# The y of a state-space layer: from four token phases on partitions to channels on partitions

## The chip, the cores and the metric

One Trainium2 chip, one of its cores. The metric is the device time of one execution in microseconds (us). Five engines of the core work beside one another and meet at semaphores: TensorE (PE, matmuls and weight loads), VectorE (DVE), ScalarE (ACT), GpSimd (POOL) and SyncE (SP, which issues the weight loads from memory).

## The reference

A streaming encoder step with two layers, for 512 prompt frames and 64 frames of a running stream (T = 576 tokens, model width 1024). Layer 0 is FFN, S5 mixer, FFN; layer 1 is FFN, differential attention, FFN; a LayerNorm stands behind each. The change touches the S5 mixer alone:

```python
def block_step(carry, u_blk):
    h_re, h_im = carry
    bu_re = jnp.einsum('gpc,btgc->btgp', bb_re, u_blk)
    ...
    _, _, hs_re, hs_im = lax.associative_scan(complex_affine_combine, (a_r, a_i, bu_re, bu_im), axis=1)
    y_blk = jnp.einsum('gcp,btgp->btgc', c_re, hs_re) - jnp.einsum('gcp,btgp->btgc', c_im, hs_im)
...
y = y.transpose(1, 0, 2, 3, 4).reshape(B, L, D_MODEL) + d_skip.astype(f32) * u
z = jax.nn.gelu(y).astype(x.dtype)
out, gate = jnp.split(z @ w_glu, 2, axis=-1)
return out * jax.nn.sigmoid(gate), h_re, h_im
```

## The kernel before, in words

**Tiles.** Activations lie with channels on partitions: `r` is 128 x 8 x 576. The tokens are worked in two halves, h = 0 with 256 tokens and h = 1 with 320. All large weight matrices pass through one numbered sequence of tiles, 128 output channels each, with K = 8 (or 7) blocks of 128 inputs. For a tile SP loads `raw` (four buffers), ACT casts it to `wh` (`act_hi`, L498, three buffers), DVE makes the rest `wl` = raw - wh (`dve_lo`, L504, three buffers), and PE does three matmuls per block (`pe_tile`, L520 to L522), 24 or 21 in all, of 256 or 320 columns. The cast and the subtraction for tile n+3 stand in ACT's and DVE's program at tile n, since a buffer is free only when PE has left it.

**Steps.** Everything else is a Python generator that is advanced by one step (`step(beside)`) behind each tile, on each engine separately; a step number is thus the same tile on all four engines, and the order on each engine is fixed by the program. `paced(work, n)` spreads a generator over n steps, `packed(work, room)` lets it run until the sizes that it yields (elements per partition plus 60 for each instruction) reach `room`, then ends the step. `idle(n)` does nothing for n steps.

**The S5 mixer** runs beside the FFN of the other token half: S5 of h = 0 beside FFN 0 of h = 1 (tiles of 320 columns), S5 of h = 1 beside FFN 1 of h = 0 (tiles of 256 columns), each behind the 12 steps of a LayerNorm. In its own steps:
- steps 0 to 3: the input is copied to `u4` with four token phases (jj) on the four partition groups of 32 (`dve_u4`, `act_u4`); the token block has BLK = 4 tokens, so there are n = 64 or 80 blocks
- steps 4 to 18: `pe_s5` multiplies block inputs (L1639), ACT copies them to `hs` (L1561)
- from step 11: `dve_scan`, the scan over the blocks on DVE (L1461 to L1472), for channel group grp = 0 and then grp = 1, each over `SCAN[h]` steps (11 for h = 0, 15 for h = 1) with `SCAN_ROOM[h]` of work in a step
- step `outputs_at(h, grp)` and the three behind it: PE makes y of one block of 128 channels, d, in each (L1656 and L1659) into bank d of the PSUM tensor `misc`. It waits for the scan (`s_sh`)
- four steps later: `dve_y` and `act_y` copy y out of PSUM to `ysb` (L1424), in 16 copies of 32 partitions, four on DVE (one in a step) and twelve on ACT (three in a step). Then ACT waits for DVE's copies (`s_yd`), does gelu on `ysb` in one instruction (L1581) and casts to `xh` (L1585); `pool_s5` makes `xl` (L1617)
- the step after the last: the gated linear unit of the mixer (`glu` tiles), which needs `xh` and `xl`.

**The y matmuls before.** For one d there are four q (32 channels each), and for each q one matmul with `tt2` on `u4` and two with `cp2` (real and imaginary) on `hs`, each with 128 stationary columns: 4 phases x 32 channels. So phase jj comes out on partitions 32jj, channel group q in columns q*n to (q+1)*n. Float32 matmuls are two instruction pairs in the trace each, so one d is 24 pairs. The moving operand of the `cp2` matmuls, `hs[:, grp, :, 0:GB, ri, 4d+q]`, takes one element out of every 32 (128 bytes apart); that of the `tt2` matmuls is contiguous.

## Time and profile before

| | |
|---|---|
| Median of 3 runs | 2335.3 us (2335.25 to 2335.64) |
| The profiled execution's own time | 2336.36 us |
| Its span in the trace | 2334.4 us |
| PE busy / weight loads (PEld) | 2247.0 / 2204.7 us |
| DVE, ACT, POOL busy | 1522.1, 1144.1, 579.9 us |
| PE clock granted, mean of the span | 0.984 of full |

The busy time of PE is the length of its matmul records, which overlap, so a busy PE need not be at its peak; but where PE is not busy nothing runs on it. Spans and shares are over the whole kernel, and the two S5 stretches (about 290 to 450 us and 590 to 815 us) have to be looked at for themselves. Durations of rows are from the start to the end of an instruction; for matmuls the distance between starts is what a stream of them costs.

### The profile page before, as it was taken

What the parts mean: (1) busy time and instruction counts of PE and PEld (TensorE: products, weight loads), DVE (VectorE), ACT (ScalarE), POOL (GpSimd) and SP (SyncE); (2) the same over time, 40 slices, a digit from 0 to 9 for tenths busy, and PEclk for the clock granted to TensorE, in tenths of its full rate; (3) what the DMA queues carried; (4) which work ended last, traced back from release to release, by engine and by line L of the source; (5) the groups of instructions that cost most, each with busy time, mean ns of one, the idle gap of its engine ahead of it and who ended that gap; (6) DMA issues with size and microseconds to landing.
All of it is one profiled execution on the core that took longest, in us unless ns stands there. A gap on an engine that the chain in (4) does not pass through costs nothing. (4 is left out here: it accounts for less than half of the span.)

```text
span 2334.4 us, 42465 instructions
## 1 busy us (share of the span) xinstructions
PE 2247.0 (96%) x17067; PEld 2204.7 (94%) x17067; DVE 1522.1 (65%) x2284; ACT 1144.1 (49%) x1923; POOL 579.9 (25%) x499
## 2 busy tenths in 40 slices
PE   8989999999998998999999999999999999899997
PEld 8989999999998998999999999999999998889997
DVE  6898768656788578444475575655687665465444
ACT  4434543555645547333365465555466554354332
POOL 2267401123211333211251123011352011141110
PEclk9999999999999999999999999999999999999999
DMA  9568675454665455555568655544555456355552
GB/s 250 166 187 239 195 218 174 128 170 132 213 215 175 139 162 145 182 152 149 149 200 277 189 159 172 154 122 137 153 155 176 136 153 184 106 152 162 145 155 79
DMA packets 705365, 391.12 MB, mean 168 GB/s; under 512 B 25001, under 2 KB 693138, under 8 KB 705170
## 3 DMA queue, kind: packets, MB, share of 16 engines
q1 hardware_dynamic: 662720, 332.44, 49.6%
q10 hardware_dynamic: 42450, 55.96, 7.2%
q8 instruction: 136, 2.23, 0.4%
q14 instruction: 59, 0.48, 0.1%
HBM read 366.53 MB, written 21.82 MB: 166 GB/s over the span
## 5 line engine op out<-in xcount | busy, mean ns | idle before, releaser
L504 DVE TENSOR_TENSOR wl<-raw,wh 128x1024 fp32r<-128x1024 f32 (+1 forms) x640 | 797.6, 1246 | 459.1 <-ACT wh L498 456.9
L520 PE MATMUL tile_ps<-xh,wh 128*128 128x256 f32 (+1 forms) x3520 | 1057.6, 300 | 26.8 <-DVE wl L504 13.7
L521 PE MATMUL tile_ps<-xl,wh 128*128 128x256 f32 (+1 forms) x3520 | 1039.2, 295 | 0.0
L522 PE MATMUL tile_ps<-xh,wl 128*128 128x256 f32 (+1 forms) x3520 | 1039.0, 295 | 0.0
L498 ACT CAST wh<-raw 128x1024 fp32r<-128x1024 f32 (+1 forms) x640 | 655.5, 1025 | 755.0 <-PE tile_ps L522 746.5
L520 PEld LDWEIGHTS tile_ps<-xh,wh 128*128 128x128 f32 x3520 | 669.9, 190 | 36.8 <-DVE wl L504 18.3
L521 PEld LDWEIGHTS tile_ps<-xl,wh 128*128 128x128 f32 x3520 | 671.1, 191 | 1.0 <-issue 0.2
L522 PEld LDWEIGHTS tile_ps<-xh,wl 128*128 128x128 f32 x3520 | 670.3, 190 | 0.0
L663 POOL TENSOR_TENSOR hl<-hf,hh 128x256 fp32r<-128x256 f32 (+1 forms) x176 | 245.1, 1392 | 1271.8 <-ACT hh L571 1271.2
L520 PE MATMUL tile_ps<-hh,wh 128*128 128x320 f32 (+1 forms) x1472 | 443.5, 301 | 7.5 <-POOL hl L663 4.3
L521 PE MATMUL tile_ps<-hl,wh 128*128 128x320 f32 (+1 forms) x1472 | 434.1, 295 | 0.0
L522 PE MATMUL tile_ps<-hh,wl 128*128 128x320 f32 (+1 forms) x1472 | 433.9, 295 | 0.0
L520 PEld LDWEIGHTS tile_ps<-hh,wh 128*128 128x128 f32 x1472 | 277.8, 189 | 12.3 <-POOL hl L663 5.5
L521 PEld LDWEIGHTS tile_ps<-hl,wh 128*128 128x128 f32 x1472 | 277.8, 189 | 0.3
L522 PEld LDWEIGHTS tile_ps<-hh,wl 128*128 128x128 f32 x1472 | 277.4, 188 | 0.0
L636 DVE SCALAR_TENSOR_TENSOR r<-r,tile_ps 128x256 f32<-128x256 f32 (+1 forms) x208 | 93.9, 452 | 142.7 <-PE tile_ps L522 141.2
L565 ACT ACTIVATE sil<-tile_ps 128x320 f32<-128x320 f32 (+1 forms) x140 | 57.6, 411 | 186.6 <-PE tile_ps L522 181.6
L613 DVE SCALAR_TENSOR_TENSOR hf<-sil,tile_ps 128x256 f32<-128x256 f32 (+1 forms) x176 | 79.4, 451 | 86.0 <-PE tile_ps L522 84.0
L571 ACT CAST hh<-hf 128x256 fp32r<-128x256 f32 (+1 forms) x176 | 75.7, 430 | 64.2 <-DVE hf L613 62.9
L825 POOL TENSOR_TENSOR xl<-r,xh 128x256 fp32r<-128x256 f32 (+1 forms) x68 | 74.7, 1118 | 92.3 <-ACT xh L738 52.6
L702 POOL TENSOR_TENSOR zc<-zc,r 128x256 f32<-128x256 f32 (+1 forms) x64 | 64.3, 1005 | 130.7 <-DVE r L636 84.1
L805 POOL TENSOR_TENSOR zq<-zq,sq 128x256 f32<-128x256 f32 (+1 forms) x54 | 62.2, 1152 | 19.3 <-ACT sq L733 13.7
(294 smaller groups left out, 1732.3 us busy)
## 6 DMA issues: line engine op xcount, KB each, us to landing
raw<-in_ffn_w_in_dram SPq DMA_DIRECT2D x352, 512.0 KB, 3.9
raw<-in_ffn_w_out_dram SPq DMA_DIRECT2D x128, 448.0 KB, 3.7
raw<-in_ffn_w_out_dram SPq DMA_DIRECT2D x64, 512.0 KB, 4.0
raw<-in_ssm_w_glu_dram SPq DMA_DIRECT2D x32, 512.0 KB, 3.9
raw<-in_attn_w_kv_dram SPq DMA_DIRECT2D x32, 512.0 KB, 3.9
wt<-scr_w ACTq DMA_DIRECT2D x16, 512.0 KB, 4.3
cp<-scr_c ACTq DMA_DIRECT2D x16, 512.0 KB, 4.1
raw<-in_attn_w_q_dram SPq DMA_DIRECT2D x16, 512.0 KB, 4.0
```

Of the source, the lines that this page charges most:

```text
L498: nc.scalar.copy(wh[n % WS][:, 0:k, :], raw[n % RAWS][:, 0:k, :]).then_inc(w_hi, 1)
L504: nc.vector.tensor_tensor(wl[n % WS][:, 0:k, :], raw[n % RAWS][:, 0:k, :], wh[n % WS][:, 0:k, :].bitcast(F32), ALU.subtract).then_inc(w_lo, 1)
L520: nc.tensor.matmul(o, wh[w][:, kk, :], xa, start=kk == 0, stop=False)
L521: nc.tensor.matmul(o, wh[w][:, kk, :], xb, start=False, stop=False)
L522: mm = nc.tensor.matmul(o, wl[w][:, kk, :], xa, start=False, stop=kk == ROWS[n] - 1)
L571: nc.scalar.copy(hh[:, i, 0:N], hf[:, 0:N]).then_inc(hh_ready, 1)
L613: nc.vector.scalar_tensor_tensor(out=hf[:, 0:N], in0=sil[:, 0:N], scalar=0.25 if (f, h, p) in TANH else 0.5, in1=bank(n + 1, h), op0=ALU.m ...
L636: nc.vector.scalar_tensor_tensor(out=r[:, d, CS[h]], in0=r[:, d, CS[h]], scalar=alpha, in1=bank(n, h), op0=ALU.mult, op1=ALU.add).then_inc ...
L663: nc.gpsimd.tensor_tensor(hl[:, i, 0:N], hf[:, 0:N], hh[:, i, 0:N].bitcast(F32), ALU.subtract).then_inc(hl_ready, 1)
L702: nc.gpsimd.tensor_tensor(zc[:, 0:N], zc[:, 0:N], r[:, d, CS[h]], ALU.add).then_inc(ln_zc, 1)
L805: nc.gpsimd.tensor_tensor(zq[:, 0:N], zq[:, 0:N], sq[d % 3][:, 0:N], ALU.add).then_inc(ln_zq, 1)
L825: nc.gpsimd.tensor_tensor(low[:, d, 0:NT[h]], r[:, d, CS[h]], high[:, d, 0:NT[h]].bitcast(F32), ALU.subtract).then_inc(x_ready[h], 1)
```

## The change: what it does

- The y matmuls have 32 stationary columns instead of 128, and the output goes to the 32 partitions of channel group q, columns jj*n to (jj+1)*n of bank d. For one d and one phase jj the four q stand side by side in four column groups of the array. Each matmul of before becomes four: 96 instruction pairs for one d instead of 24.
- The 16 copies of a turn are gone on both engines (`y_copy`, `dve_y`, the semaphores `s_yd` and `s_ya`). ACT's gelu reads bank d of PSUM and writes `ysb`, one instruction for each d, four behind one another in one step; it reorders (j b) to (b j) as it writes. PE's waits for the copies become waits for gelu (`s_ge`).
- `SCAN` goes from (11, 15) to (13, 17) steps and `SCAN_ROOM` from (1800, 1620) to (1520, 1430). y's first step moves two steps later for grp = 0 and four for grp = 1; the casts and POOL's part of grp = 1 stay at their steps, the length of S5 (`s5_steps`) stays 47 and 55.

PE, one d of h = 1. The rows of before, word for word from the order of PE's instructions (x2 counts calls of the program, each of which is two instruction pairs):

```order
L522 MATMUL tile_ps<-hh,wl_61 128x256
L1656 MATMUL misc<-u_122,tt_1_130 128x80
L1659 MATMUL misc<-hs,cp_1_126 128x80 x2
L1656 MATMUL misc<-u_122,tt_1_130 128x80
L1659 MATMUL misc<-hs,cp_1_126 128x80 x2
L1656 MATMUL misc<-u_122,tt_1_130 128x80
L1659 MATMUL misc<-hs,cp_1_126 128x80 x2
```

and of the change:

```order
L522 MATMUL tile_ps<-hh,wl_63 128x256
L1633 MATMUL misc<-u_122,tt_1_130 32x80 x4
L1639 MATMUL misc<-hs,cp_1_126 32x80 x8
L1633 MATMUL misc<-u_122,tt_1_130 32x80 x4
L1639 MATMUL misc<-hs,cp_1_126 32x80 x8
L1633 MATMUL misc<-u_122,tt_1_130 32x80 x4
L1639 MATMUL misc<-hs,cp_1_126 32x80 x8
```

The same piece of work comes four times as often, at a quarter of the width.

ACT, h = 1, grp = 0, from the first copy of y to gelu, before (`wh` is the cast for the tile three ahead):

```order
L1424 COPY ysb<-misc 32x320 x3
L498 CAST wh_59<-raw_57 128x896
L1424 COPY ysb<-misc 32x320 x3
L498 CAST wh_60<-raw_54 128x1024
L1424 COPY ysb<-misc 32x320 x3
L498 CAST wh_58<-raw_55 128x1024
L1424 COPY ysb<-misc 32x320 x3
L498 CAST wh_59<-raw_56 128x1024
L1581 ACT_TABLE_LOAD
L1581 ACTIVATE ysb<-ysb 128x1280
```

and of the change:

```order
L498 CAST wh_60<-raw_54 128x1024
L1528 DMA cp_3_128<-scr_c 128x1024
L1529 DMA tt_3_132<-scr_t 128x512
L1557 ACT_TABLE_LOAD
L1557 ACTIVATE ysb<-misc 128x4x80 x4
L498 CAST wh_58<-raw_55 128x1024
L1563 CAST xh_51<-ysb 128x320 x2
```

Twelve copies are gone from between the casts, and four gelus stand together between two of them.

DVE, h = 1, grp = 1, two neighbouring tiles in the middle of the scan, before:

```order
L636 SCALAR_TENSOR_TENSOR r<-r,tile_ps 128x256
L504 TENSOR_TENSOR wl_62<-raw_57,wh_59 128x896
L1461 TENSOR_TENSOR sa_137<-hs,lam_85 128x160
...
L1470 TENSOR_TENSOR hs<-hs,sb_139 128x2x32
L1424 COPY ysb<-misc 32x320
L636 SCALAR_TENSOR_TENSOR r<-r,tile_ps 128x256
L504 TENSOR_TENSOR wl_63<-raw_54,wh_60 128x1024
```

and of the change, about the same place of the scan:

```order
L636 SCALAR_TENSOR_TENSOR r<-r,tile_ps 128x256
L504 TENSOR_TENSOR wl_62<-raw_56,wh_59 128x896
L1454 TENSOR_TENSOR sb_139<-hs,lam_85 128x5x16
L1456 TENSOR_TENSOR sb_139<-hs,lam_85 128x5x16
L1458 TENSOR_TENSOR hs<-hs,sa_137 128x5x32
...
L1452 TENSOR_TENSOR sa_137<-hs,lam_86 128x32
L504 TENSOR_TENSOR wl_63<-raw_57,wh_60 128x1024
```

The copy between the scan's instructions and the next tile's is gone. The diff:

```diff
--- before.py
+++ after.py
@@ -1397,36 +1397,27 @@
         s_sh = sem("block_states")
         s_carry = sem("prompt_states_kept")
         s_ym = sem("y_multiplied")
-        s_yd = sem("y_copied_dve")
-        s_ya = sem("y_copied_act")
         s_ge = sem("gelu_done")
         s_fin = sem("final_states")
         s_st = sem("states_transposed")
         s_so = sem("states_copied")
 
 
-        SCAN = (11, 15)
+        SCAN = (13, 17)
         INPUTS = 4
 
         def outputs_at(h, grp):
             return 12 + (grp + 1) * SCAN[h]
 
         def s5_steps(h):
-            return outputs_at(h, 1) + 13
+            return outputs_at(h, 1) + 9
 
         def u4_copy(eng_copy, done, h, half, jj, q):
             src = r[32 * q:32 * q + 32, 4 * half:4 * half + 4, CS[h]][:, :, jj::BLK]
             eng_copy(u4[32 * jj:32 * jj + 32, 4 * half:4 * half + 4, q, 0:NBLK[h]], src).then_inc(done, 1)
 
-        def y_copy(eng_copy, done, h, jj, q):
-            n = NBLK[h]
-            dst = ysb[32 * q:32 * q + 32, :, 0:NT[h]][:, :, jj::BLK]
-            eng_copy(dst, misc[32 * jj:32 * jj + 32, :, q * n:(q + 1) * n]).then_inc(done, 1)
-
         U4_DVE = ((0, 0), (0, 1), (0, 2), (0, 3), (1, 0), (1, 1), (1, 2), (1, 3), (2, 0), (2, 1))
         U4_ACT = ((2, 2), (2, 3), (3, 0), (3, 1), (3, 2), (3, 3))
-        Y_DVE = ((0, 0), (0, 1), (0, 2), (0, 3))
-        Y_ACT = tuple((jj, q) for jj in (1, 2, 3) for q in range(4))
 
         def tables_stored(eng):
             for stored, parts in ((s_tdw, 1), (s_tdc, 1), (s_tdt, BLK)):
@@ -1508,22 +1499,12 @@
             elif h:
                 eng.wait_ge(x_ready[0], X_GELU + 8)
 
-        def dve_y(dve, h, grp):
-            turn = 2 * h + grp + 1
-            dve.wait_ge(s_ym, 4 * turn)
-            ysb_free(dve, h, grp)
-            for jj, q in Y_DVE:
-                y_copy(nc.vector.tensor_copy, s_yd, h, jj, q)
-                yield
-
         def dve_s5(dve, h):
             scans = chained(idle(11), paced(packed(dve_scan(dve, h, 0), SCAN_ROOM[h]), SCAN[h]),
                             paced(packed(dve_scan(dve, h, 1), SCAN_ROOM[h]), SCAN[h]))
-            return paced(together(dve_u4(dve, h), scans,
-                                  chained(idle(outputs_at(h, 0) + 4), dve_y(dve, h, 0)),
-                                  chained(idle(outputs_at(h, 1) + 4), dve_y(dve, h, 1))), s5_steps(h))
-
-        SCAN_ROOM = (1800, 1620)
+            return paced(together(dve_u4(dve, h), scans), s5_steps(h))
+
+        SCAN_ROOM = (1520, 1430)
 
         def act_u4(act, h):
             tables_stored(act)
@@ -1569,19 +1550,16 @@
                 yield
 
         def act_y(act, h, grp):
-            turn = 2 * h + grp + 1
-            act.wait_ge(s_ym, 4 * turn)
+            turn = 2 * h + grp
             ysb_free(act, h, grp)
-            for k, (jj, q) in enumerate(Y_ACT):
-                y_copy(nc.scalar.copy, s_ya, h, jj, q)
-                if k % 3 == 2:
-                    yield
-            act.wait_ge(s_yd, len(Y_DVE) * turn)
-            act.wait_ge(s_ya, len(Y_ACT) * turn)
-            nc.scalar.activation(ysb[:, :, 0:NT[h]], ysb[:, :, 0:NT[h]], ACT.Gelu_apprx_tanh).then_inc(s_ge, 1)
-            yield
-            act.wait_ge(s_ge, turn)
             for d in range(4):
+                act.wait_ge(s_ym, 4 * turn + d + 1)
+                nc.scalar.activation(ysb[:, d, 0:NT[h]].rearrange("p (b j) -> p j b", j=BLK),
+                                     misc[:, d, 0:NT[h]].rearrange("p (j b) -> p j b", j=BLK),
+                                     ACT.Gelu_apprx_tanh).then_inc(s_ge, 1)
+            yield
+            for d in range(4):
+                act.wait_ge(s_ge, 4 * turn + d + 1)
                 nc.scalar.copy(xh[h][:, 4 * grp + d, :], ysb[:, d, 0:NT[h]]).then_inc(xh_ready[h], 1)
                 if d % 2:
                     yield
@@ -1610,8 +1588,8 @@
         def pool_s5(pool, h):
             at = 0
             for grp in range(2):
-                yield from idle(outputs_at(h, grp) + 9 - at)
-                at = outputs_at(h, grp) + 11
+                yield from idle(outputs_at(h, grp) + 5 - at)
+                at = outputs_at(h, grp) + 7
                 for d in range(4 * grp, 4 * grp + 4):
                     pool.wait_ge(xh_ready[h], X_GELU + d + 1)
                     nc.gpsimd.tensor_tensor(xl[h][:, d, :], ysb[:, d % 4, 0:NT[h]], xh[h][:, d, :].bitcast(F32),
@@ -1629,8 +1607,7 @@
                     pe.wait_ge(s_u4d, len(U4_DVE) * (2 * h + dt // 4 + 1))
                     pe.wait_ge(s_u4a, len(U4_ACT) * (2 * h + dt // 4 + 1))
                 if dt == 0 and h:
-                    pe.wait_ge(s_yd, 2 * len(Y_DVE))
-                    pe.wait_ge(s_ya, 2 * len(Y_ACT))
+                    pe.wait_ge(s_ge, 8)
                 pe.wait_ge(s_wl[s], 16 * (DT // 2 * h + dt // 2 + 1))
                 if dt >= 2:
                     pe.wait_ge(s_wc, 2 * (DT * h + dt - 1))
@@ -1647,25 +1624,27 @@
                 pe.wait_ge(s_sh, 2 * h + grp + 1)
                 pe.wait_ge(s_wc, 2 * DT * (h + 1))
                 if grp:
-                    pe.wait_ge(s_yd, len(Y_DVE) * (2 * h + 1))
-                    pe.wait_ge(s_ya, len(Y_ACT) * (2 * h + 1))
+                    pe.wait_ge(s_ge, 8 * h + 4)
                 for d in range(4):
                     pe.wait_ge(s_bl[d], 32 * (2 * h + grp + 1))
-                    for q in range(4):
-                        o = misc[:, d, q * n:(q + 1) * n]
-                        nc.tensor.matmul(o, tt2[d][:, q, :], u4[:, 4 * grp + d, q, 0:n], start=True, stop=False,
-                                         skip_group_check=True)
+                    for jj in range(BLK):
+                        c = slice(32 * jj, 32 * jj + 32)
+                        for q in range(4):
+                            nc.tensor.matmul(misc[32 * q:32 * q + 32, d, jj * n:(jj + 1) * n], tt2[d][:, q, c],
+                                             u4[:, 4 * grp + d, q, 0:n], start=True, stop=False,
+                                             skip_group_check=True)
                         for ri in range(2):
-                            mm = nc.tensor.matmul(o.rearrange("p (g i) -> p g i", i=GB), cp2[d][:, ri, q, :],
-                                                  hs[:, grp, 0:NGRP[h], 0:GB, ri, 4 * d + q],
-                                                  start=False, stop=ri == 1, skip_group_check=True)
+                            for q in range(4):
+                                o = misc[32 * q:32 * q + 32, d, jj * n:(jj + 1) * n]
+                                mm = nc.tensor.matmul(o.rearrange("p (g i) -> p g i", i=GB), cp2[d][:, ri, q, c],
+                                                      hs[:, grp, 0:NGRP[h], 0:GB, ri, 4 * d + q],
+                                                      start=False, stop=ri == 1, skip_group_check=True)
                     mm.then_inc(s_ym, 1)
                     yield
-            yield from idle(6)
+            yield from idle(2)
             if h:
                 pe.wait_ge(s_fin, 8)
-                pe.wait_ge(s_yd, 4 * len(Y_DVE))
-                pe.wait_ge(s_ya, 4 * len(Y_ACT))
+                pe.wait_ge(s_ge, 16)
                 for k in range(4):
                     nc.tensor.transpose(misc[0:NPAIR, 0, k * P:(k + 1) * P], hlast[:, k % 2, k // 2, :],
                                         ident[:]).then_inc(s_st, 1)
```

## Rows read from the trace of the kernel before

**Rows 1.** The page: busy time by engine, share of the span.
```profile
PE 2247.0 (96%) x17067; PEld 2204.7 (94%) x17067; DVE 1522.1 (65%) x2284; ACT 1144.1 (49%) x1923; POOL 579.9 (25%) x499
```

**Rows 2.** Windows: stretch, its length, then busy time by engine, PE clock, DMA.
```profile
404.00:434.00 30.00, 26.41 (x180) 25.64 (x178) 27.36 (x61) 18.55 (x26) 5.67 (x4) 1.00 0.50 147
652.00:704.00 52.00, 50.11 (x426) 49.26 (x424) 49.79 (x87) 22.69 (x38) 9.00 (x7) 1.00 0.65 198
734.00:768.00 34.00, 26.88 (x193) 25.68 (x192) 33.03 (x60) 18.89 (x28) 9.86 (x7) 0.90 0.42 120
785.00:800.00 15.00, 13.59 (x115) 13.38 (x114) 7.29 (x9) 10.24 (x16) 2.65 (x2) 1.00 0.32 93
```

**Rows 3.** Timeline of PE where a wait ended: start, length, [idle before <-releaser].
```profile
742.38 0.38 PE L520 MATMUL tile_ps<-xh,wh 128*128 128x256 f32 x1 [2.65 <-DVE wl L504]
796.38 0.38 PE L520 MATMUL tile_ps<-hh,wh 128*128 128x256 f32 x1 [1.41 <-POOL hl L663]
```

**Rows 4.** Timeline of DVE behind which PE waited at 742.38.
```profile
739.70 0.32 DVE L1461 TENSOR_TENSOR sa<-hs,lam 128x160 f32<-128x160 f32 x1
740.03 0.71 DVE L1424 COPY ysb<-misc 32x320 f32<-32x320 f32 x1
740.77 0.42 DVE L636 SCALAR_TENSOR_TENSOR r<-r,tile_ps 128x256 f32<-128x256 f32 x1
741.11 1.22 DVE L504 TENSOR_TENSOR wl<-raw,wh 128x1024 fp32r<-128x1024 f32 x1
```

**Rows 5.** The tile ysb: min/median/max ns of its instructions, and waits.
```profile
L1424 ACT COPY ysb<-misc x48: 612/670/746, 408.1 to 802.7; 32x256 f32<-32x256 f32 x24, 32x320 f32<-32x320 f32 x24
L1424 DVE COPY ysb<-misc x16: 595/666/727, 412.4 to 802.4; 32x256 f32<-32x256 f32 x8, 32x320 f32<-32x320 f32 x8
L1581 ACT ACTIVATE ysb<-ysb x4: 1061/1167/1275, 426.1 to 805.7; 128x1024 f32<-128x1024 f32 x2, 128x1280 f32<-128x1280 f32 x2
```

**Rows 6.** Timeline of PE, one d of y, h = 1 and then h = 0.
```profile
709.36 0.28 PE L522 MATMUL tile_ps<-hh,wl 128*128 128x256 f32 x1
709.48 0.34 PE L1656 MATMUL misc<-u,tt 128*128 128x80 f32 x2
...
710.21 0.36 PE L1656 MATMUL misc<-u,tt 128*128 128x80 f32 x2
...
712.38 0.39 PE L520 MATMUL tile_ps<-hh,wh 128*128 128x256 f32 x1
```
```profile
381.60 0.31 PE L520 MATMUL tile_ps<-xh,wh 128*128 128x320 f32 x1
...
382.03 0.33 PE L1656 MATMUL misc<-u,tt 128*128 128x64 f32 x2
...
382.67 0.36 PE L1656 MATMUL misc<-u,tt 128*128 128x64 f32 x2
...
384.63 0.40 PE L520 MATMUL tile_ps<-xh,wh 128*128 128x320 f32 x1
```

**Rows 7.** Timeline of PE at 133 us: matmuls in four column groups.
```profile
132.64 0.60 PE L1327 MATMUL misc<-ident,ebuf 128*128 128x128 f32 x4
133.16 0.65 PE L1315 MATMUL misc<-cp,ebuf 128*32 128x128 f32 x16
133.63 0.24 PE L1319 MATMUL misc<-skip,ident 128*32 128x32 f32 x8
133.80 0.38 PE L520 MATMUL tile_ps<-xh,wh 128*128 128x256 f32 x1
```

**Rows 8.** Timeline of PE, block inputs of h = 1, contiguous, full width.
```profile
636.64 0.28 PE L520 MATMUL tile_ps<-hh,wh 128*128 128x256 f32 x1
...
636.99 1.91 PE L1639 MATMUL misc<-u,wt 128*128 128x80 f32 x16
638.69 0.36 PE L520 MATMUL tile_ps<-hh,wh 128*128 128x256 f32 x1
```

**Rows 9.** A window at the halved PE clock, columns as in rows 2.
```profile
744.00:746.00 2.00, 2.00 (x11) 2.00 (x11) 1.94 (x5) 0.86 (x1) 0.00 (x0) 0.50 0.71 210
```

## The prediction

> **What bounds the kernel now.** The page comes first: PE has work in 96% of the span [rows 1], so the kernel is bound by TensorE, and a change can give back only PE's own time or the gaps in it. The windows of the two S5 stretches come next, because there alone the change acts. Four windows hold PE's gaps: 3.59, 1.89, 7.12 and 1.41 us not busy, 14.0 us in all [rows 2]. In the first three DVE is busy 27.36 of 30, 49.79 of 52 and 33.03 of 34 us: VectorE bounds these stretches, not TensorE. The third also has a mean granted clock of 0.90, that is 3.4 us lost in 34; the window at 744 us, behind a wait of PE, shows 0.50, which is 1.2 of 2.4 GHz [rows 9]. Last the timeline, for what the gaps wait on. At 742.38 PE had been idle for 2.65 us until DVE's `wl` [rows 3], and DVE went without a pause from scan to y copy (0.71 us) to residual add to `wl` (1.22 us) [rows 4]. At 796.38 it waited 1.41 us for POOL's `hl`, which comes from a cast on ACT, and ACT had three y copies ahead of that cast (`act_y` puts three in a step, 670 ns each [rows 5]).
>
> **DVE's side of the change.** Removed: 16 copies of 666 ns [rows 5], 10.7 us. Those of grp 0 (four for each half, 2.6 us for h = 0, 2.9 us for h = 1) lie in the scan of grp 1, where DVE has no room. Those of grp 1 lie behind the scan and free nothing that is short. Moved: the scans do the same work in two more tiles each. A tile of 24 matmuls lasts 24 x 0.117 = 2.8 us at 256 columns (start to start from 636.64 to 636.99 [rows 8]) and 24 x 0.145 = 3.5 us at 320 [rows 6]. DVE's own work in it is one `wl`, 1.22 us, and in every second tile an operation like the 0.42 us one [rows 4]. So a further tile gives the scan 2.8 - 1.22 - 0.21 = 1.4 us for h = 1, and 2.0 us for h = 0.
>
> - h = 0, window 1: 2.6 us of copies and 2 x 2.0 us of room are more than the 3.59 us of gaps. All of it goes: **-3.6 us**. Here I also count the wait of y for the scan, since the scan gets its last work done earlier against y's step.
> - h = 1, grp 0, window 2: no copies in it, 2 x 1.4 = 2.8 us of room for 1.89 us of gaps. But the new `SCAN_ROOM` of 1430 does not thin the scan's first steps, whose single instructions are larger than either room, and they fall on tiles of 21 matmuls. I take a little over half: **-1.1 us**.
> - h = 1, grp 1, window 3: lost are 7.1 us of gaps and 3.4 us of clock, 10.5. Given back are 2.9 us of copies and 2.8 us of room, 5.7 us. I take **-5.5 us**. A DVE that is short sets the time of such a stretch whichever way PE spends it, so the clock is not counted a second time. What is late next: still `wl`, about 5 us in small waits.
> - window 4: the three copies ahead of the cast are gone, and gelu stands where `hl` is already made: **-1.4 us**.
>
> **ACT's side.** Removed: 48 copies of 670 ns and 4 gelus of 1.17 us, 36.8 us. Added: 16 gelus that read PSUM and write with a stride. No row shows that. The copies have the same count of elements, source and stride and take 612 to 746 ns; the gelu without a stride took 1061 ns for 1024 elements [rows 5]. Bounds: 0.4 and 1.0 us each. I take the copy's 0.7. ACT is idle for half of this stretch, so the saving is worth nothing by itself. What is new is a block of 1.3 us of table load (as before) and 4 x 0.7 us between two casts of `wh`. That cast is made three tiles ahead. From the end of tile k: cast 1.0, block 4.1, cast 1.0, `wl` 1.1 to 1.2, sum 7.3 us, against three tiles of 21 matmuls, 7.4 us for h = 1 and 9.1 us for h = 0. It just fits: **+0.3 us** for both turns of h = 1; with 1.0 us gelus it would be +2.4 us. Before, ACT waited there for the last copy of DVE; that wait goes too, and nobody was waiting for it alone. The loads of `cp2` and `tt2` move with y and keep their distance to it; casts, POOL's part and `glu` keep their steps.
>
> **PE's side, the open point.** Now one d costs from the last tile matmul to the next 712.38 - 709.36 = 3.02 us for h = 1; for h = 0, with 0.145 us of distance to the last one, 384.63 - 382.03 + 0.14 = 2.74 us. Inside, six pairs take 0.73 us (709.48 to 710.21) and 0.64 us (382.03 to 382.67) [rows 6]. The contiguous operand at 80 columns costs 1.70 / 16 = 0.106 us a pair [rows 8], so the strided pairs cost (0.75 - 0.21) / 4 = 0.135 us for h = 1 (0.75 is the mean of the four q) and 0.112 us for h = 0.
>
> After the change 96 pairs must pass. Column groups are shown at 133 us: 16 pairs of 128 contiguous columns, 32 wide, start within 0.47 us, and with the 8 short ones all is over in 0.64 us [rows 7]. Had they gone one by one, 16 pairs at the full-width rate of 0.106 us would need 1.7 us. So four run at once, in rounds of four pairs of about 0.11 us for 128 columns, 0.86 ns a column. One d then has 8 rounds of contiguous and 16 of strided operands. Contiguous: 8 x 80 x 0.86 ns = 0.55 us (h = 1), 0.44 us (h = 0). Strided, if each of the four streams keeps the pace that it has alone: 16 x 0.135 = 2.16 us, and 16 x 0.112 = 1.79 us. Going into the narrow mode and out: the stretch from the last transpose (132.64 + 3 x 0.11) to 133.80 is 0.83 us for 0.5 us of rounds, so 0.33 us. Sum: 3.04 us for h = 1 (no change) and 2.56 us for h = 0 (-0.18). Eight of each: **-1.1 us** with the fractions. That is the lower bound of the cost. The upper one, if the four strided streams share one reader and pass one after another: 64 x 0.135 + 0.55 + 0.33 = 9.5 us and 64 x 0.112 + 0.44 + 0.33 = 7.9 us a d, +6.5 and +5.2, so +94 us. I take the lower one, being nearest to the only row with four groups. It shows four different moving operands at full pace, but contiguous ones.
>
> The Trainium skill, "TensorEngine Tiling (Array Packing)", Key Properties, speaks against the change: switching the tiling mode drains TensorE, here 16 times each way. The row at 133 us agrees and prices both switches together with the start-up at 0.33 us, against 0.10 to 0.18 us of such overhead in the present form (3.02 less four times 0.73, 2.74 less four times 0.64); the difference, some 0.2 us a d, is +3 us, and it is in the sum; without it PE would give back 4 us.
>
> **Sum.** -3.6 - 1.1 - 5.5 - 1.4 + 0.3 - 1.1 = -12.4 us. The profiled span of 2334.4 becomes 2322.0; the execution around it took 2336.4, and the median of the runs is 1.1 us below that, 2335.3. So 2335.3 - 12.4 = **2322.9, say 2323 us**.
>
> **The rivals.**
> 1. *The strided streams get in each other's way* (slower). Place: the `cp2` rounds, 256 of them over the kernel. The four q of one round read neighbouring elements of the same rows of `hs`, 128 bytes apart from column to column. For it: a lone strided stream is already slower than a contiguous one at 80 columns, 0.135 against 0.106 us, so its reads are the limit. Against it: four contiguous streams keep pace. Price at half pace: 128 rounds x 0.112 + 128 x 0.135 = +31.6 us on PE, while the longer steps let DVE catch up by some 3 more: 2323 + 32 - 3, about 2351 us. It decides from a round of 0.16 us for h = 0 and 0.20 us for h = 1 on (+12 us). One after another: about 2323 + 95 = 2418 us.
> The Trainium skill, "SBUF — State Buffer", the note on cachelines, has the rule: lines of 16 bytes, and each access to a new line pays. The 0.135 against 0.106 us agree with it. It does not say whether four streams pay side by side; if they queue for the line, it gives this rival.
> 2. *The supply of instructions.* Now 24 pairs in 2.6 us, then 96 in the same time. The densest stretch of the trace is 24 pairs in 0.64 us, 27 ns a pair [rows 7]; at that pace 96 take 2.6 us, and h = 0 gains nothing. Only a longer run could show that the pace does not hold. If it fell to the 0.106 us of the full-width stream, one d would take 10 us, and the whole some 2323 + 115 = 2438 us.
> 3. *The shortage of DVE only moves.* The scan is not less work; grp 1 of h = 1 now runs two tiles longer beside the same `wl`s, and POOL slows DVE where both run. Then the two further tiles give nothing and only the copies count: -2.6 - 2.9 - 1.4 + 0.3 - 1.1 = -7.7, less some 4 us of new small waits and a stretch or two at the halved clock: 2332 us, no change.
>
> **How the numbers follow.** About 0.2% (4.7 us) is what a measurement of this kernel can tell from no change, so faster is below 2330.6 and slower above 2340. The forecast has 0.66; the streams at half pace or thereabouts 0.18; all one by one or starved of instructions 0.06; the moved shortage 0.10. The forecast's own range: all gaps and the clock back (-14.0 - 3.4 - 1.1) gives 2316.8; with rounds some 10% longer and gelu at 1.0 us it is 2330. To hold the time 8 times in 10 the range has to reach to the half pace: 2316 to 2351. Faster 0.68 (with a little of rival 3), same 0.09, slower 0.23.
>
> **What would show it.** The `cp2` matmuls should start in rounds of four, a round every 0.11 (h = 0) or 0.135 us (h = 1); one d from tile to tile in 2.6 and 3.0 us. The windows of 404 to 434 us should have no gap over 0.5 us, those of h = 1's second scan some 3 to 5 us, still behind `wl`, with at most one stretch at half clock. The waits of ACT for DVE's copies and of PE for `hl` at 796 us should be gone. The gelus should take 0.6 to 0.75 us. The forecast is wrong if a d takes over 4 us, or if the gaps behind `wl` keep their 12 us.

## The result, and the profile after

The changed kernel takes 2344.28 us (median of 6 runs, 2340.73 to 2346.69), the kernel before 2335.28 us in the same comparison (6 runs, 2334.14 to 2336.63). The ratio is 1.0043, with a 95% interval of 1.0034 to 1.0053: slower by 9 us, where 12.4 us less were forecast. The profiled span is 2341.7 us against 2334.4, so 7.3 us more, and that is the sum to be explained below.

The page's busy line of the kernel after, to be read against [rows 1]: PE has 14.4 us more work, DVE 7.3 us less, ACT 27.1 us less.

```profile
PE 2261.4 (97%) x18219; PEld 2209.4 (94%) x18219; DVE 1514.8 (65%) x2268; ACT 1117.0 (48%) x1887; POOL 575.0 (25%) x499
```

The windows of [rows 2] after the change, with the two whole S5 stretches below them (columns: stretch, length, then busy time of PE, PEld, DVE, ACT, POOL, the granted PE clock, DMA):

```profile
404.00:434.00 30.00, 29.35 (x269) 28.07 (x268) 22.12 (x55) 11.58 (x17) 3.51 (x4) 1.00 0.52 161
652.00:704.00 52.00, 50.49 (x430) 49.89 (x429) 47.21 (x88) 22.40 (x38) 8.23 (x6) 1.00 0.68 208
734.00:768.00 34.00, 30.32 (x271) 29.29 (x263) 27.50 (x64) 15.74 (x24) 7.26 (x7) 0.90 0.51 154
785.00:800.00 15.00, 15.00 (x273) 13.65 (x269) 4.61 (x6) 3.75 (x6) 2.45 (x2) 1.00 0.43 125
290.00:450.00 160.00, 158.72 (x1468) 155.16 (x1467) 116.30 (x197) 61.82 (x94) 18.16 (x15) 1.00 0.60 182
590.00:830.00 240.00, 227.92 (x2362) 218.84 (x2362) 175.18 (x281) 107.68 (x157) 46.22 (x38) 0.98 0.61 181
```

The same two stretches of the kernel before:

```profile
290.00:450.00 160.00, 156.41 (x1134) 155.64 (x1133) 116.06 (x201) 67.44 (x101) 19.44 (x14) 1.00 0.60 182
590.00:830.00 240.00, 226.31 (x1839) 223.35 (x1840) 184.77 (x298) 123.74 (x178) 48.36 (x38) 0.98 0.62 185
```

Windows fixed in time hold other tiles once the program has slipped, and the second long window of before begins inside a gap. So here is the same piece of the program in both traces, from one `wl` ahead of the first S5 stretch to one behind the second (in both traces they are the same two instructions), before and after:

```profile
291.68:828.26 536.58, 513.81 (x3962) 508.34 (x3961) 379.86 (x597) 271.58 (x403) 109.55 (x90) 0.98 0.59 175
289.19:837.89 548.70, 531.50 (x5113) 515.95 (x5113) 372.76 (x582) 243.97 (x367) 104.88 (x90) 0.99 0.58 171
```

It grew by 12.1 us: PE is busy 17.7 us longer and idle for 17.2 instead of 22.8 us, so its gaps shrank by 5.6 us. What PE waited for in the second stretch (590 to 830 us) before the change:

```profile
PE tile_ps L520 <- DVE wl L504: 7.9, 7, 2.6
PE tile_ps L520 <- POOL hl L663: 1.4, 1, 1.4
PE misc L1656 <- DVE hs L1472: 1.0, 2, 0.7
```

After it, the waits for `hl` and for the scan (`hs`; 1.7 us more of these in the first stretch) are gone, 4.1 us together. Those behind `wl`, which the change was made for, only fell from 7.9 to 7.5 us, and from 1.8 to 1.2 us in the first stretch. The third window keeps its mean clock of 0.90, and PE, though busier, got less of the program done.

Where PE's time went, a timeline of PE shows in the form of [rows 6]: one d of y, first h = 1, then h = 0. The first row of each piece is the last tile matmul ahead of y, the last one the first tile matmul behind it.

```profile
718.80 0.28 PE L522 MATMUL tile_ps<-hh,wl 128*128 128x256 f32 x1
719.00 0.35 PE L1633 MATMUL misc<-u,tt 128*32 128x80 f32 x8
719.17 1.04 PE L1639 MATMUL misc<-hs,cp 128*32 128x80 f32 x16
719.96 0.39 PE L1633 MATMUL misc<-u,tt 128*32 128x80 f32 x8
...
723.11 0.38 PE L520 MATMUL tile_ps<-hh,wh 128*128 128x256 f32 x1
```
```profile
393.42 0.31 PE L522 MATMUL tile_ps<-xh,wl 128*128 128x320 f32 x1
393.66 0.32 PE L1633 MATMUL misc<-u,tt 128*32 128x64 f32 x8
393.80 0.88 PE L1639 MATMUL misc<-hs,cp 128*32 128x64 f32 x16
...
397.01 0.41 PE L520 MATMUL tile_ps<-xh,wh 128*128 128x320 f32 x1
```

One d takes 723.11 - 718.80 = 4.31 us for h = 1 and 397.01 - 393.42 = 3.59 us for h = 0, against 3.02 and 2.74 us before: 8 x (1.29 + 0.85) = **+17.1 us**. The contiguous rounds (L1633) are short. The 16 strided matmuls (L1639) last from 719.17 to 719.96 until the next phase begins, 0.79 us for four rounds and the start of the next. Taken over all of them, a strided round of four starts every 0.205 us for h = 1 and every 0.167 us for h = 0 (medians of the times from a matmul to the fourth behind it, within the stretches of 16), where 0.135 and 0.112 us were forecast.

So +17.1 on PE and -5.6 of gaps make +11.5 of the 12.1 us. The whole span grew by only 7.3 us, because the rest of the kernel, which the change doesn't touch, came out 4.8 us shorter in this execution than in the one profiled before: some 1.5 us less idle time of PE, and fewer stretches at half clock. (The mean granted clock of the whole span rose from 0.984 to 0.986, 37.4 us lost before, 2334.4 x 0.016, and 32.8 after; from 590 to 830 us it is 0.98 in both.) That part is a difference between executions and no merit of the change.

**A new wait.** The longest gap of PE beside the scans is now at 752.87, as long as the one of [rows 3] that it replaces. Timeline of four engines ahead of it (start, length, engine; in brackets the idle time before it and its releaser):

```profile
739.58 1.05 ACT L498 CAST wh<-raw 128x1024 fp32r<-128x1024 f32 x1 [5.83 <-PE tile_ps L522]
740.64 1.28 ACT L1557 ACT_TABLE_LOAD   x1
741.94 2.53 ACT L1557 ACTIVATE ysb<-misc 128x320 f32<-128x320 f32 x4
744.23 1.09 ACT L498 CAST wh<-raw 128x1024 fp32r<-128x1024 f32 x1
745.35 1.23 DVE L504 TENSOR_TENSOR wl<-raw,wh 128x1024 fp32r<-128x1024 f32 x1 [1.88 <-ACT wh L498]
745.75 4.48 POOL L1595 TENSOR_TENSOR xl<-ysb,xh 128x320 fp32r<-128x320 f32 x4 [40.53 <-ACT xh L1563]
746.50 1.00 DVE L1454 TENSOR_TENSOR sb<-hs,lam 128x160 f32<-128x160 f32 x1
...
751.60 1.21 DVE L504 TENSOR_TENSOR wl<-raw,wh 128x1024 fp32r<-128x1024 f32 x1
752.87 0.58 PE L520 MATMUL tile_ps<-xh,wh 128*128 128x256 f32 x1 [2.78 <-DVE wl L504]
...
762.92 0.32 DVE L1454 TENSOR_TENSOR sb<-hs,lam 128x160 f32<-128x160 f32 x1
```

The table load and the four gelus stand between two casts of `wh`; DVE loses 1.88 us waiting for the second; then its scan works beside POOL's `xl`, and an operation of 160 elements takes 1.00 us where the same one takes 0.32 us at 762.92, with POOL idle; `wl` is late and PE waits 2.78 us. PE then runs at half clock (0.50), as it did behind the wait of [rows 9]:

```profile
752.00:755.00 3.00, 2.13 (x10) 2.14 (x11) 2.79 (x12) 2.99 (x4) 0.00 (x0) 0.50 0.30 84
```

The gelus themselves came out as forecast, a median of 728 ns for 0.7 us:

```profile
L1557 ACT ACTIVATE ysb<-misc x16: 629/728/822, 416.3 to 815.8; 128x256 f32<-128x256 f32 x8, 128x320 f32<-128x320 f32 x8
```

**A DVE with time in the wrong place.** The waits of DVE from 652 to 772 us, the scans of h = 1, after the change (us in total, times, longest):

```profile
DVE r L636 <- PE tile_ps L522: 12.5, 4, 3.9
DVE wl L504 <- ACT wh L498: 6.2, 7, 1.9
```

and one of the four, in the timeline of DVE at the second d of y:

```profile
721.21 1.48 DVE L1461 TENSOR_TENSOR hs<-hs,sb 128x1280 f32<-128x1280 f32 x1
725.95 0.42 DVE L636 SCALAR_TENSOR_TENSOR r<-r,tile_ps 128x256 f32<-128x256 f32 x1 [3.26 <-PE tile_ps L522]
```

DVE, which I had called the bound of these stretches, waits 12.5 us for PE here: 2.3 us at 652.33, ahead of the scan, and 10.2 us (3.26, 3.92 and 3.06) in three of the four steps that hold a d of y and so last 7 us. It is short of time some 10 us later. (Before the change the same view shows 3.8 us in three waits.) `packed` hands each step of the scan the same room, whatever the step lasts.

### The profile page after: what moved, and what is told of

The parts are those of the page before. It is cut to its first block and busy times, and to the rows that moved or that the text cites. A ratio compares the mean times of both kernels' runs of the same rounds, so it can differ in the third digit from the quotient of the medians.

```text
span 2341.7 us, 44711 instructions
## 1 busy us (share of the span) xinstructions
PE 2261.4 (97%) x18219; PEld 2209.4 (94%) x18219; DVE 1514.8 (65%) x2268; ACT 1117.0 (48%) x1887; POOL 575.0 (25%) x499
```

## The experiments

All ratios are against the kernel before, run on the same chip in the same job.

**1. Which half of the change costs.** The change, its scans put back:

```
-        SCAN = (13, 17)
+        SCAN = (11, 15)
-        SCAN_ROOM = (1520, 1430)
+        SCAN_ROOM = (1800, 1620)
```

> The changed kernel with the scan's old steps and room (11, 15; 1800, 1620), so the new y path alone. Theory A (PE pays 0.84 us more for each of the 8 d of h = 0 and 1.28 us more for each of h = 1, 17 us in all; the two further scan steps give back only a little): about 2 to 4 us slower than the changed kernel, 2346 to 2348 us. Rival B (the two further steps are what costs, the new y path is about free): 2333 to 2337 us. PE's stretch for one d stays at 3.6 and 4.3 us under A and under B alike.

Measured: 2347.62 us (4 runs, 2346.27 to 2351.69), ratio 1.0056 (1.0039 to 1.0073). The new path of y by itself costs 13 us, as theory A says; the two further steps of the scan give back some 3 us of them (the intervals overlap), not the 9.6 us of room that the prediction built on (2 x 2.0 for h = 0 and twice 2 x 1.4 for h = 1). The edit also makes S5 four steps shorter (43 and 51 instead of 47 and 55), since its length follows from `SCAN`. PE's waits say what the steps do: over both stretches those behind `wl` are 7.6 us here, 8.7 us in the changed kernel and 9.7 us before, so the further steps don't shorten them. What they take away is PE's wait for the scan (2.3 us here, none after the change) and the one for `hl`, for here the table load and the four gelus stand ahead of the cast that `hl` needs:

```profile
808.58 0.58 PE L520 MATMUL tile_ps<-hh,wh 128*128 128x256 f32 x1 [2.73 <-POOL hl L663]
```

**2 and 3. What the strided streams meet.** In the first kernel the moving operand of `cp2` is a contiguous run of `hs` of the same length, in the second it keeps its stride but the four q of a round read states four apart instead of neighbours. Both compute y from other elements of the state than the layer asks for.

```
-    hs[:, grp, 0:NGRP[h], 0:GB, ri, 4 * d + q]
+    k = (16 * ri + 4 * d + q) * n
+    hs[:, grp].rearrange("p g i r q -> p (g i r q)")[:, k:k + n]
```
```
-    hs[:, grp, 0:NGRP[h], 0:GB, ri, 4 * d + q]
+    hs[:, grp, 0:NGRP[h], 0:GB, ri, 4 * q + d]
```

> The moving operand of the cp2 matmuls is a contiguous run of hs of the same length instead of every 32nd element, so y is computed from other elements of the state; instructions, waits and widths are the same. Theory A (four strided streams share one reader, 0.64 ns an element, so a round of four takes 0.16 and 0.20 us): the rounds fall to 0.055 and 0.069 us, one d to about 1.9 us for h = 0 and 2.1 us for h = 1 from tile to tile, PE gives back some 8 x 1.7 + 8 x 2.2 = 31 us, time about 2313 to 2318 us. Rival B (supply of instructions, about 32 to 40 ns a pair, or the writes of four column groups to PSUM): one d stays at 3.6 and 4.3 us and the time at 2344 us.

> The four streams of a round read states 4q + d instead of 4d + q: same stride, but the four elements lie 16 bytes apart instead of side by side, so y is computed from other states. Theory A1 (each read costs a turn of a shared reader, wherever it lies): rounds stay at 0.16 and 0.20 us. Theory A2 (the four get in each other's way because they want the same few bytes): rounds fall to 0.11 and 0.135 us, one d to about 2.6 and 3.1 us. Theory A3 (side by side they already share reads): rounds become longer, up to 0.22 and 0.27 us.

Measured: contiguous 2312.67 us (2312.26 to 2315.7), ratio 0.9906 (0.9891 to 0.9921); four apart 2328.38 us, one run. The timeline of PE, one d of h = 1, contiguous:

```profile
776.11 0.28 PE L522 MATMUL tile_ps<-hh,wl 128*128 128x256 f32 x1
...
776.48 0.46 PE L1641 MATMUL misc<-hs,cp 128*32 128x80 f32 x16
...
778.12 0.39 PE L520 MATMUL tile_ps<-hh,wh 128*128 128x256 f32 x1
```

and with the states four apart:

```profile
783.87 0.28 PE L522 MATMUL tile_ps<-hh,wl 128*128 128x256 f32 x1
784.07 0.35 PE L1633 MATMUL misc<-u,tt 128*32 128x80 f32 x8
784.24 0.73 PE L1639 MATMUL misc<-hs,cp 128*32 128x80 f32 x16
...
786.97 0.38 PE L520 MATMUL tile_ps<-hh,wh 128*128 128x256 f32 x1
```

With the states four apart the numbers are those of the forecast: 3.10 us a d (forecast 3.04), 2.61 us for h = 0 (2.56), a strided round every 0.137 and 0.110 us (0.135 and 0.112). Nothing differs from the changed kernel but which element each of four streams reads: elements 4 bytes apart against elements 16 bytes apart, with the same stride of 128 bytes, the same instructions, the same banks written. The time itself is that of a single run, but experiment 7 shows the same rounds and the gain, with four. So the cause of the 17 us is neither the supply of instructions (the contiguous kernel gets its 96 pairs through in 2.0 us) nor the change of mode, nor the writes, but that four streams read the same small neighbourhood of `hs` at once. How the memory makes them wait isn't shown.

**4. How the price grows with the number that share.** States 8 * (q // 2) + 2 * d + q % 2: two and two are neighbours.

> The changed kernel, the four streams of a round reading states 8*(q//2) + 2*d + q%2: two of them read neighbouring elements, the other two neighbouring elements 32 bytes further (other states than the reference's are summed, so y is another). Theory A2a, the reads of one 16-byte neighbourhood pass one after another, about 0.64 ns an element as in the rounds of 0.167 and 0.205 us: two of them take 1.3 ns for one element of each stream, less than the 1.4 to 1.7 ns that a lone strided stream takes, so the round is back at about 0.112 and 0.138 us, one d 2.6 and 3.1 us, the time about 2328. Theory A2b, a neighbourhood that two streams share costs a fixed extra whatever their number: the round stays at or near 0.167 and 0.205 us, 2344. In between, 0.13 to 0.15 and 0.16 to 0.18 us, would say that all four pass one reader and that only the number of different lines counts.

Measured: 2332.72 us (10 runs, 2330.06 to 2334.76), ratio 0.9989 (0.9980 to 0.9999). One d of h = 1 takes 716.69 - 713.30 = 3.39 us:

```profile
713.30 0.28 PE L522 MATMUL tile_ps<-hh,wl 128*128 128x256 f32 x1
...
713.67 0.82 PE L1639 MATMUL misc<-hs,cp 128*32 128x80 f32 x16
...
716.69 0.38 PE L520 MATMUL tile_ps<-hh,wh 128*128 128x256 f32 x1
```

The rounds are 0.122 us (h = 0) and 0.153 us (h = 1): 0.012 and 0.016 us above those that share nothing, where four that share stand 0.057 and 0.068 above. Neither A2a's full recovery nor A2b's fixed price, and a little below the bounds of the third reading (0.13 and 0.16 us). Four neighbours cost over four times what two and two cost; the law behind it stays open. That sharing costs, and that it grows faster than the number of streams, is what these three points show.

**5. The block of gelus.** One gelu a step from the first d on, `yield` moved into the loop and `act_y` started three steps earlier (for grp = 1 likewise):

```
-            yield
+                yield
             for d in range(4):
                 act.wait_ge(s_ge, 4 * turn + d + 1)
...
-        chained(idle(outputs_at(h, 0) + 4), act_y(act, h, 0)),
+        chained(idle(outputs_at(h, 0) + 1), act_y(act, h, 0)),
```

> One gelu in each of the four steps behind y instead of four in one step. Theory C (the wait of 2.8 us at 753 us and the halved clock behind it come from the block of 3.8 us of gelu between two casts of wh): this wait and the clock stretch go, 3 to 6 us faster than the changed kernel, 2338 to 2341 us. Rival D (it comes from the scan on DVE, slowed by POOL, as before the change): the wait stays within 0.5 us and the time at 2343 to 2345 us.

Measured: 2342.41 us (6 runs, 2340.95 to 2347.23), ratio 1.0040 (1.0025 to 1.0055), no difference from the change that can be told. The wait did as theory C says, the time as D says. The 3.06 us from matmul to matmul at 752.87 become 1.11 us and the half clock behind it goes, but PE's waits for `wl` from 680 to 830 us stay the same in sum, only in more pieces. After the change, and then with the gelus apart:

```profile
PE tile_ps L520 <- DVE wl L504: 7.5, 10, 2.8
```
```profile
PE tile_ps L520 <- DVE wl L504: 7.5, 12, 1.5
```

The block set the place and the length of the longest gap, not what the gaps come to.

**6. A layout with unit stride.** `hs` stored with the token index innermost, so that both y and the block inputs' copy see contiguous runs:

```
-        hs = sm("hs", [P, 2, max(NGRP), GB + 1, 2, GB])
+        hs = sm("hs", [P, 2, max(NGRP), 2, GB, GB + 1])[:].rearrange("p a g r q i -> p a g i r q")
...
```

> The changed kernel, the whole computation, with hs stored so that the 16 blocks of a group lie side by side for each state: PE's moving operand is runs of 16 contiguous elements, while DVE's scan and ACT's copies stride. Theory A: one d falls to 1.8 and 2.1 us, PE gives back about 30 us. If DVE reads with a stride of 68 bytes at the same pace: about 2314 us. If a strided scan costs DVE twice its time (31 us more for h = 1), DVE sets the time of both S5 stretches and the kernel takes 2350 to 2380 us.

Measured: 2341.79 us (7 runs, 2340.69 to 2345.2), ratio 1.0028 (1.0017 to 1.0040), between the two forecasts. y has its speed: the d at 804 us takes 2.05 us. The scan pays. The same operation group of DVE from 590 to 830 us in the changed kernel, then in this one (ns min/median/max):

```profile
L1458 DVE TENSOR_TENSOR hs<-hs,sa x24: 191/408/1494, 659.7 to 778.4; 128x32 f32<-128x32 f32 x6, 128x1280 f32<-128x1280 f32 x4, 128x640 f32<-128x640 f32 x4, 128x320 f32<-128x320 f32 x4
```
```profile
L1458 DVE TENSOR_TENSOR hs<-hs,sa x24: 216/594/2535, 659.2 to 786.4; 128x32 f32<-128x32 f32 x6, 128x1280 f32<-128x1280 f32 x4, 128x640 f32<-128x640 f32 x4, 128x320 f32<-128x320 f32 x4
```

and PE's waits from 680 to 800 us:

```profile
PE tile_ps L520 <- DVE wl L504: 25.1, 14, 3.4
```

The stride was not got rid of but moved, from PE, where it costs 0.07 us a round (0.137 against the contiguous kernel's 0.069), to an engine that has no time to spare in these steps.

**7. The states permuted.** As in 3, but with the computation whole: column 4q + d of `hs` now holds pair 4d + q. The copy of the block inputs writes there, and the small tables, the initial and the final states are permuted to match; gelus apart as in 5.

```
-    nc.scalar.copy(hs[:, dt // 4, 0:G, 1:GB + 1, ri, 4 * (dt % 4):4 * (dt % 4) + 4],
+    nc.scalar.copy(hs[:, dt // 4, 0:G, 1:GB + 1, ri, dt % 4::4],
...
-    hs[:, grp, 0:NGRP[h], 0:GB, ri, 4 * d + q],
+    hs[:, grp, 0:NGRP[h], 0:GB, ri, 4 * q + d],
```

> The whole computation, with one gelu a step, and the state stored in another order: position 4q + d of hs holds pair 4d + q, so the four streams of a round read 16 bytes apart. Theory A2 (streams that want the same few bytes queue): one d takes 2.6 us for h = 0 and 3.1 us for h = 1 from tile to tile, against 3.57 and 4.32 us; PE gives back 8 x 0.97 + 8 x 1.22 = 17.5 us, less a microsecond or two that the scan then lacks: about 2326 us, faster than the kernel before by 0.4%. Rival (the gain of the run with other states came from its wrong data or elsewhere): 2342 us.

Measured: 2323.59 us (4 runs, 2322.07 to 2324.09), ratio 0.9947 (0.9932 to 0.9962): 18.8 us below the kernel of 5, whose only other difference is the permutation. A d takes 782.19 - 779.09 = 3.10 us (782.19 is the first tile matmul behind it). The price is on ACT, where the copy now writes single elements:

```profile
L1550 ACT COPY hs<-misc x32: 631/741/837, 306.9 to 674.2; 128x256 f32<-128x256 f32 x16, 128x320 f32<-128x320 f32 x16
```

741 ns for 395 ns in the changed kernel, 32 x 0.35 = 11 us, on an engine that had them to spare.

**8. The room of a scan step.** `packed` takes a list: large room where a step of the scan lasts long or comes early, small room behind.

```
 def packed(work, room):
-    used = 0
+    rooms = iter(room)
+    used, room = 0, next(rooms)
     for size in work:
         used += size
         if used >= room:
             used -= room
+            room = next(rooms, 1e9)
             yield
...
-        SCAN_ROOM = (1520, 1430)
+        SCAN_ROOM = ([1520] * 13, [2400] * 4 + [1100] * 9), \
+                    ([1430, 2100, 1500, 2100, 1200, 2100, 1200, 2100] + [1220] * 9, [3300] * 4 + [820] * 13)
```

First on the permuted kernel, then on the changed kernel as it is:

> As the permuted kernel, and the scan's room varies with what PE does beside it: large in the steps with block inputs or y on PE, small in the others. Theory E (the gaps that the two further steps did not remove are steps in which wl and the even share of the scan are more than a tile, while DVE idles some 12 us in the four steps with y): the gaps behind wl of h = 1 fall from 8 to 3 us or less and no clock is lost there, 5 to 8 us faster than the permuted kernel, 2318 to 2321 us. Rival F (the scan lacks DVE time in total): within 2 us of the permuted kernel.

> The changed kernel with the varying room alone. Theory E: 5 to 9 us faster than the changed kernel, 2335 to 2339 us, with PE's 3.6 and 4.3 us for one d unchanged. Rival F: 2342 to 2345 us.

Measured: 2313.98 us (4 runs, 2312.31 to 2317.42), ratio 0.9909 (0.9892 to 0.9925); and 2333.88 us (10 runs, 2330.56 to 2335.05), ratio 0.9995 (0.9986 to 1.0005). Each is 10 us below its like. In the second, DVE's waits for PE from 652 to 772 us, 12.5 us in the changed kernel, are now

```profile
DVE r L638 <- PE tile_ps L524: 1.7, 1, 1.7
```

**9 and 10. The same room without the new y.** The kernel before, with `packed` as in 8 and a list of rooms for its 11 and 15 steps, and then with 13 and 17 steps and the list of 8, its y path and copies kept:

```
-        SCAN_ROOM = (1800, 1620)
+        SCAN_ROOM = ([1800] * 11, [2600] * 4 + [1300] * 7), \
+                    ([1430, 2100, 1500, 2100, 1200, 2100, 1200, 2100] + [1450] * 7, [3300] * 4 + [960] * 11)
```

> The kernel BEFORE, whole and with its own 11 and 15 scan steps; only the even room of a scan step is replaced by a list: large where steps of the scan meet tiles with y or early tiles with slack, small behind them. Two theories of where the gain of about 10 us comes from that the same edit gave in the changed kernel. E: the scan was badly spread over its steps, whichever way y is computed; then before also gains most of its 14 us of gaps and 3.4 us of clock, I expect 7 to 12 us, 2324 to 2328 us. G: only the two further steps make the varied room possible, because with 11 and 15 steps and 16 y copies on VectorE there is more work than time; then under 4 us, 2331 to 2335, and the gaps behind wl stay in the second scan of h = 1.

> The kernel BEFORE with its y path and copies as they are, its scans taking 13 and 17 steps, with the same varied room as the two kernels with it. One d of y stays at 2.74 and 3.02 us. Set against the changed kernel with that room (2333.9 us) it tells what the new y path alone is worth, with sign; against the one with permuted states (2314.0 us) whether the new path is worth anything once its streams don't share lines. If the y path costs its 17 us of TensorE and gives back only copies, I expect about 2320 us here: 14 below the former. If VectorE's 10.7 us of y copies bind, 2325 or more, and the permuted one stays some 10 us ahead of it.

Measured: 2322.17 us (5 runs, 2319.86 to 2324.84), ratio 0.9952 (0.9938 to 0.9966); and 2334.16 us (11 runs, 2330.9 to 2336.02), ratio 1.0002 (0.9993 to 1.0010). E holds: the kernel before lacked no steps and no time of DVE for these 11 us, its scan was badly spread. My guess for the second was 14 us off. The two further steps do harm while the old y tail of 13 steps follows them: the timeline of PE shows y's last product late at the next layer, a wait of 4.11 us that the kernel of 9 doesn't have,

```profile
811.43 0.64 PE L522 MATMUL tile_ps<-xh,wh 128*128 128x320 f32 x1 [4.11 <-POOL xl L1619]
```

and the mean clock from 812 to 818 us is 0.66. For h = 0 there is a like one:

```profile
486.45 0.38 PE L522 MATMUL tile_ps<-xh,wh 128*128 128x256 f32 x1 [2.54 <-POOL xl L1619]
```

The two waits and the clock behind them make up some 10 of the 12 us between the two kernels. With this tail the further steps make S5 51 and 59 steps long, four more than before. Set beside the changed kernel with the same steps and the same rooms (experiment 8, 2333.9 us), the time is the same: there PE pays its 17 us, here the long tail and the copies stand against them. The shorter tail of the change (9 steps) is what makes room for the further steps at all; they are no edit by themselves.

**11. The further steps with everything else in place.** The permuted kernel with 11 and 15 steps and the rooms of 9:

> The kernel with permuted states, spread gelus and varied room (2314.0 us), its scans put back to 11 and 15 steps, with the room that the kernel before had in its own varied form (2322.2 us). Theory H: once the room is varied the two further steps are worth little, since the steps of the scan that were too full were so because of the spread; then within 3 us of 2314, and the gain of 8 us over the kernel before with varied room is that of the y path. Theory I: the further steps are worth the 2.8 us of room each half that I had forecast, on both groups; then 2318 to 2322 us, with waits for wl of 5 to 8 us more in the second half's scans.

Measured: 2318.46 us (5 runs, 2315.33 to 2319.57), ratio 0.9927 (0.9914 to 0.9939). Against 0.9909 the two steps are worth about 4 us, at the edge between H and I; the intervals overlap. But the mechanism of I doesn't hold: from 590 to 830 us PE waits 2.8 us for `wl` against 2.2 with the further steps, not 5 to 8 us more. The further steps take away 1.0 us of waiting for `hl` and 0.7 us for the scan. Against the kernel before with the same steps and the same rooms (0.9952) the new path of y with the permutation, its shorter tail and gelus apart gains 4 to 6 us.

## Why the prediction was wrong

**The step that failed** is the term "Strided, if each of the four streams keeps the pace that it has alone". It made -1.1 us of PE's side (-1.3, if its terms are added exactly); measured are +17.1 us, and experiment 3 gives back the forecast's rounds by moving the streams 16 bytes apart. I had taken the lower bound because the only row with four groups [rows 7] lies nearest, and had written beside it that its operands are contiguous: I chose by the form of the instruction (four groups) and passed over the one property that differed (stride and shared neighbourhood). Rival 1 was this case; its condition for deciding, rounds of 0.16 and 0.20 us and +12 us, is nearly the measured 0.167 and 0.205 us. It got 0.18. That the measured time lies inside the range of 2316 to 2351 us is owed to this rival, to which the range was stretched; the forecast itself, 12.4 us faster, has the wrong sign.

The Trainium skill, "SBUF — State Buffer", the note on cachelines, gives lines of 16 bytes and a penalty for each access to a new line. The experiments agree with its line size so far as 16 bytes apart is free and 4 bytes apart is not. They show what it doesn't say: that streams running at once are slower when they read the same 16 bytes than when each reads 16 bytes of its own.

**The rest, step by step.**

- Contiguous rounds at 0.86 ns a column and the switching of 0.33 us: right. The contiguous kernel does a d of h = 1 in 2.0 us, and the sum of all terms for h = 1 is 3.10 for 3.04 us in experiment 3. Rival 2, the supply of instructions, is out.
- Window 1, -3.6: 26.41 to 29.35 us busy, so 2.9, nearly right. Window 4, -1.4: right to the digit.
- Windows 2 and 3, -1.1 and -5.5: 0.4 and 3.4 us of PE's idle time in the same windows, with the halved clock still there, and new small waits behind 768 us; from 590 to 830 us the waits behind `wl` fell by 0.4 us in all. The two S5 stretches together gave 5.6 us for the 11.6 of the four windows, and 4.1 of the 5.6 are the waits for the scan and for `hl`. The fault is the sentence "VectorE bounds these stretches": a mean busy share of 27 of 30 and 33 of 34 us came from the steps that are too full, while other steps of the same scans leave DVE waiting (3.8 us for h = 1 before the change, 10.2 after it). A further step has 1.4 us of room only if the work is put where the room is. Rival 3, in which the steps give nothing, was nearer; what it took for a lack of time was a lack of spread.
- The ACT block, +0.3: "it just fits" was wrong at one of its places. DVE waited 1.88 us for the cast and the longest gap came from there. Spreading it out moved the time no more than can be measured (experiment 5), so on the whole its price was small after all, for another reason than mine: the gaps only split.
- The gelus at 0.7 us, the lost waits for y copies and for `hl`: right.

**By experiments, the whole account** (ratios to before): new y path alone 1.0056; with further steps 1.0043; with the rooms spread 0.9995; with gelus apart and states permuted 0.9909, that is 2314.0 us. The best that the old y path reached is 0.9952, 2322.2 us. So the change, with its states in another order, is worth 8 to 10 us (4 to 6 of them the new y path, about 4 the further steps), its memory pattern cost 16 to 19, and some 10 us lay in something that it left alone, the even room of `packed`.

## What to carry to other kernels

Four column groups multiply the reads of the moving operand by four: before trusting the pace of one stream, look at which bytes the four read at the same moment, and order the data so that they lie 16 bytes or more apart. When VectorE looks full over a stretch, list its waits in that stretch too; time that it spends waiting for TensorE in some steps is worth more than steps added at the end, and costs only a table of numbers. A path that looks worse than before may be a good path with one bad operand: the kernel of experiment 7 is faster than both, and what it changed is the order of one index (and the steps of the gelus, which by experiment 5 are worth nothing that can be told).

## What the runs showed of the hardware that was not expected

- Four strided streams of 128 bytes stride, read at once: a round takes 0.110 / 0.137 us (64 / 80 elements) when they are 16 bytes apart, 0.122 / 0.153 when two and two are neighbours, 0.167 / 0.205 when all four are. The first is the pace of a single such stream; so four unshared ones cost nothing.
- The supply of instructions kept up with 96 pairs in 2.0 us, 21 ns a pair with both switches of mode, where the densest stretch known before had 27 ns [rows 7].
- A strided operand is dear on DVE: the scan's operations of 1280 elements took up to 2.5 us instead of 1.5 when the inner stride of `hs` was 17 elements instead of 1 (experiment 6), without POOL beside them.
- With POOL's `xl` beside it, a DVE operation of 160 elements took 1.00 us instead of 0.32. That POOL slows DVE was in the prediction, threefold was not. What is added doesn't grow with the operation: in the trace after the change, operations of the scan that meet work of POOL take 0.86 or 1.00 us instead of 0.32 (160 elements), 1.02 instead of 0.48 (320) and 2.02 instead of 1.49 (1280). So it is 0.5 to 0.7 us each, threefold for the shortest and a third more for the longest. Not every operation beside POOL pays, and no run took POOL's work away to test it.
